# Conditioning projections of a two-layer decoder step: raw float32 slabs in four TensorE column groups in place of split slabs over the whole array

## The chip, the core and the metric

The kernel runs as one program on one core of a Trainium2 chip. The metric is the device time of one execution in microseconds (us). The engines are named as the profile names them: PE is TensorE (PEld its weight loads), DVE is VectorE, ACT is ScalarE, POOL is GpSimd, and SP is the queue that issues most DMAs. A number such as L649 is a line of the kernel before.

## What is computed

One inference step of a decoder trunk with D = 1024, for a prompt of 512 tokens and 8 single-token samples, hence 520 token columns and 9 sequences (each with its own conditioning vector c). Layer 0 mixes tokens with a gated linear recurrence of 8 heads (HGRN2), layer 1 with latent attention over a shared latent. Around each mixer stand two half-step SwiGLU networks of inner width 2816. Every sub-layer is an RMS norm whose shift, scale and gate come from c:

```
sc = jax.nn.silu(c)
for l in range(DEPTH):
    if l == N_A_LAYERS:
        ckv, krope = shared_kv(x, sc, pos, kv_w_ada, kv_b_ada, ...)     # its own shift and scale, 2 x D columns
    mods = (sc @ w_ada[l] + b_ada[l]).reshape(Bn, 3, 3, D)[:, :, :, None, :]
    def mod(y, j):
        return rmsnorm(y, g_norm[l, j]) * (1 + mods[:, j, 1]) + mods[:, j, 0]
    x = x + 0.5 * mods[:, 0, 2] * swiglu(mod(x, 0), w_ffn_gu[l, 0], w_ffn_down[l, 0])
    h = mod(x, 1)
    ...                                    # y = HGRN2 (layer 0) or latent attention (layer 1)
    x = x + mods[:, 1, 2] * y
    x = x + 0.5 * mods[:, 2, 2] * swiglu(mod(x, 2), w_ffn_gu[l, 1], w_ffn_down[l, 1])
```

The conditioning projections `sc @ w_ada[l]` (9 x 1024 columns in each layer) and `sc @ kv_w_ada` (2 x 1024 columns) are what is changed. They read 80 MiB of the weights for a result of 9 rows.

## The kernel before

**Slabs.** All weights are float32 and come through a ring of four buffers, `raw` (`RAW` = 4), in slabs of up to 2048 words in each of 128 partitions, 1 MiB (1.05 MB). SP issues the two DMAs of a slab (L408) once the slab four places earlier has been multiplied (`slot_used`). ACT then makes `w_hi`, the slab rounded to the float32r type, and DVE makes `w_lo`, what is left of it (L1239, L1635). Both run `AHEAD` = 2 slabs ahead of the multiplication: handling slab k they first split slab k + 2. ACT waits for the landing there, and everything behind that wait on ACT waits with it.

**Large products.** The activations are split the same way (`hn_hi`, `hn_lo`, `hid_hi`, `hid_lo`). A 128 x 128 weight tile is multiplied with 520 columns in two halves of 260, each in three passes, hi x hi, hi x lo and lo x hi (L627 to L629).

**Conditioning slabs (`ada`).** There are 80: 36 of each `w_ada[l]` and 8 of `kv_w_ada`, each 256 columns wide with all 1024 rows. silu(c) stands in `sc18`, 128 partitions x 8 chunks x 18 columns, high part of the 9 sequences beside the low part. One slab takes 16 matmuls of 256 moving columns (L649 with `w_hi`, L650 with `w_lo`), which accumulate 18 rows in PSUM bank 6. ACT copies the rows to `rows` (L1247), and `ada_comb` on PE (L661) adds the two parts and turns the rows to columns by two matmuls against a constant. DVE adds the bias into `mods` (L1643). So each slab has its own rows copy, turn and bias step.

**Where they stand.** 14 slabs (`ADA_FIRST`) go in front of the first norm. One stands behind each of the 22 hidden chunks of the two networks of layer 0 (its turn lies in the next hidden chunk, between gate and up). Two go with each of the 8 heads' projections, which run interleaved with the recurrence of the head before (`hgrn_events`). The last 6 go with the head norms, which run in the last head's recurrence (`last_events`, `hgrn_norm`). The two networks of layer 1 have none. The order on each engine is written out by hand; the engines run the same list of events and meet at semaphores.

## Time and profile before

| what | value |
|---|---|
| median of 3 runs | 2860.28 us |
| range | 2857.2 to 2860.41 us |
| span of the profiled execution | 2860.2 us |
| PE busy / DVE / ACT | 92% / 45% / 31% |
| PE's share of the chain that ended last | 84% |
| mean granted clock, share of full speed | 0.958 |
| moved by DMA | 294.25 MB, mean 103 GB/s |

The profile is of one execution, and its span equals the median to 0.1 us. Its busy times of PE add overlapping records, since matmuls are pipelined: what one costs is seen from the distance between starts, not from its own duration. A float32 matmul (not float32r) leaves two weight-load records and two matmul records.

### The profile page before, as it was taken

How to read it: one execution, taken by the hardware profiler on the slowest of the kernel's cores; microseconds unless marked ns; L12 is line 12 of the kernel's file. 1: busy time of each engine (PE TensorE's matmuls, PEld its weight loads, DVE VectorE, ACT ScalarE, POOL GpSimd, SP SyncE). 2: the span in 40 equal slices, each digit the busy share in tenths (PEclk: the TensorE clock that was granted, in tenths of full speed). 3: DMA queues.
4: the chain of work that ended last, by engine and by line, in shares of the span. 5: the costliest groups of instructions: out<-in, count | busy, mean ns of one | idle time of the engine just before them, and what ended most of it. 6: DMA issues, size and time to landing. Idle time of an engine off the chain costs nothing.

```text
span 2860.2 us, 48702 instructions
## 1 busy us (share of the span) xinstructions
PE 2621.6 (92%) x20002; PEld 2407.8 (84%) x20002; DVE 1296.3 (45%) x1975; ACT 881.4 (31%) x1034; POOL 38.2 (1%) x64
## 2 busy tenths in 40 slices
PE   5799999899998689999987999996888999899997
PEld 4799999899998589999987999996763437899997
DVE  5544344556566854434446333345452223533333
ACT  4533133433334243313325212124333222321212
POOL 1000000000000000000000000000000000000000
PEclk9899999999999699999998999998999998999998
DMA  8344353333444125434432323221023332223321
GB/s 270 111 148 142 108 153 122 104 108 104 120 119 140 60 81 152 143 104 140 136 107 59 99 78 100 78 89 28 27 85 88 88 91 59 74 81 95 91 75 57
DMA packets 412517, 294.25 MB, mean 103 GB/s; under 512 B 35557, under 2 KB 408380, under 8 KB 412384
## 3 DMA queue, kind: packets, MB, share of 16 engines
q1 hardware_dynamic: 407456, 277.14, 32.6%
q0 software_dynamic: 4928, 15.30, 1.7%
q8 instruction: 88, 1.44, 0.2%
q14 instruction: 45, 0.37, 0.0%
HBM read 284.87 MB, written 7.51 MB: 102 GB/s over the span
## 4 chain that ended last, share of the span: by engine, by line
PE 84%; DVE 7%; ACT 3%; DMA 2%; issue 2%; SPq 1%; POOL 0%; DVEq 0%; ACTq 0%; POOLq 0%
PE ps L627 22%; PE ps L628 22%; PE ps L629 22%; PE ps L649 2%; PE ps L650 2%; PE ps L1173 2%; PE ps L870 2%; PE ps L1132 2%; PE ps L661 1%; PE ps L1133 1%; DMA raw<-in_hg_w_in 1%; DMA raw<-in_w_ada 1%; DVE rstd L1694 1%; DVE rstd L1899 1%; PE ps L1106 1%
## 5 line engine op out<-in xcount | busy, mean ns | idle before, releaser
L627 PE MATMUL ps<-hn_hi,w_hi 128*128 128x260 f32 x3680 | 1066.1, 290 | 49.4 <-DVE hn_lo L1710 47.1
L629 PE MATMUL ps<-hn_hi,w_lo 128*128 128x260 f32 x3680 | 1051.5, 286 | 0.0
L628 PE MATMUL ps<-hn_lo,w_hi 128*128 128x260 f32 x3680 | 1050.6, 285 | 0.0
L627 PEld LDWEIGHTS ps<-hn_hi,w_hi 128*128 128x128 f32 x3680 | 706.3, 192 | 55.4 <-issue 51.6
L1635 DVE TENSOR_TENSOR w_lo<-raw,w_hi 128x2048 fp32r<-128x2048 f32 (+5 forms) x280 | 564.3, 2016 | 316.7 <-ACT w_hi L1239 316.6
L629 PEld LDWEIGHTS ps<-hn_hi,w_lo 128*128 128x128 f32 x3680 | 706.0, 192 | 0.0
L628 PEld LDWEIGHTS ps<-hn_lo,w_hi 128*128 128x128 f32 x3680 | 705.8, 192 | 0.0
L1239 ACT ACTIVATE w_hi<-raw 128x2048 fp32r<-128x2048 f32 (+3 forms) x273 | 472.7, 1732 | 491.8 <-DMA raw<-in_w_ffn_gu 220.8
L628 PE MATMUL ps<-hid_lo,w_hi 128*128 128x260 f32 x1408 | 398.7, 283 | 0.0
L627 PE MATMUL ps<-hid_hi,w_hi 128*128 128x260 f32 x1408 | 397.9, 283 | 0.0
L629 PE MATMUL ps<-hid_hi,w_lo 128*128 128x260 f32 x1408 | 397.8, 283 | 0.0
L1723 DVE TENSOR_TENSOR hf<-ps,sg 128x520 f32<-128x520 f32 x88 | 61.6, 700 | 487.4 <-PE ps L629 487.4
L629 PEld LDWEIGHTS ps<-hid_hi,w_lo 128*128 128x128 f32 x1408 | 265.1, 188 | 0.0
L627 PEld LDWEIGHTS ps<-hid_hi,w_hi 128*128 128x128 f32 x1408 | 264.9, 188 | 0.1
L628 PEld LDWEIGHTS ps<-hid_lo,w_hi 128*128 128x128 f32 x1408 | 264.4, 188 | 0.0
L1311 ACT ACTIVATE sg<-ps 128x520 f32<-128x520 f32 x88 | 52.6, 597 | 394.2 <-PE ps L629 394.2
L649 PE MATMUL ps<-w_hi,sc 128*18 128x256 f32 x640 | 158.3, 286 | 0.5 <-DVE x L1942 0.5
L650 PE MATMUL ps<-w_lo,sc 128*18 128x256 f32 x640 | 156.6, 284 | 0.0
L1737 DVE TENSOR_TENSOR t<-ps,gate 128x8 f32<-128x8 f32 x80 | 13.4, 167 | 255.6 <-PE ps L629 255.6
L1282 ACT ACTIVATE sq<-x 128x520 f32<-128x520 f32 x56 | 35.5, 638 | 253.8 <-DVE x L1742 212.9
L1247 ACT ACTIVATE rows<-ps 18x256 f32<-18x256 f32 x80 | 29.4, 368 | 240.0 <-PE ps L650 240.0
L870 PE MATMUL ps<-qs,kk 128*128 128x128 f32 x512 | 74.4, 292 | 26.7 <-DVE qs L1857 16.9
(289 smaller groups left out, 2357.4 us busy)
## 6 DMA issues: line engine op xcount, KB each, us to landing
raw<-in_w_ffn_gu SPq DMA_DIRECT2D x176, 512.0 KB
raw<-in_w_ada SPq DMA_DIRECT2D x144, 512.0 KB
raw<-in_w_ffn_down SPq DMA_DIRECT2D x96, 384.0 KB
raw<-in_hg_w_in SPq DMA_DIRECT2D x32, 512.0 KB
pg<-in_cache_ckv SPq DMA_DIRECT2D x128, 128.0 KB, 2.0
raw<-in_w_ffn_down SPq DMA_DIRECT2D x32, 256.0 KB
raw<-in_kv_w_ada SPq DMA_DIRECT2D x16, 512.0 KB
ss<-in_state_hgrn POOLq DMA_DIRECT2D x8, 512.0 KB, 7.1
```

The costliest lines, as they stand in the source:

```text
L627: pe.matmul(out[:, t, :], wh, xh[:, c], start=start, stop=False)
L628: pe.matmul(out[:, t, :], wh, xl[:, c], start=False, stop=False)
L629: mm = pe.matmul(out[:, t, :], wl, xh[:, c], start=False, stop=stop)
L649: pe.matmul(ps[0:18, 6, 0:ADA_W], sc18[:, k, :], hi[:, k, :], start=(k == 0), stop=False)
L650: mm = pe.matmul(ps[0:18, 6, 0:ADA_W], sc18[:, k, :], lo[:, k, :], start=False, stop=(k == 7))
L870: mm = pe.matmul(out[:, s], kk[:, q, s], qs[:, q, s], start=True, stop=True)
L1132: pe.matmul(o, qsamp[:, q, r, :], cts[g % 2][:, r, :], start=(r == 0), stop=False)
L1173: pe.matmul(ps[0:H, 3, 0:KV], pts[:, p, :], pg[q][:, p, :], start=(p == 0), stop=False)
L1239: act.activation(w_hi[:, r, 0:n], raw[r][:, 0:n], ACT.Copy).then_inc(hi_done, 1)
L1311: act.activation(two(sg[:, T.n.get("up", 0) % 2, :]), pair[0], ACT.Silu).then_inc(gate_read, 1)
L1635: ins = dve.tensor_tensor(w_lo[r][:, c], raw[r][:, c], w_hi[:, r, c], ALU.subtract)
L1723: dve.tensor_tensor(two(hf[:]), pair[1], two(sg[:, T.n.get("up", 0) % 2, :]), ALU.mult).then_inc(up_read, 1)
```

## The change

The 80 conditioning slabs are no longer split. A slab is now 256 rows (`ADA_K` = 2 chunks of 128) by all 1024 columns of one of the 20 blocks of D columns, four slabs to a block. PE multiplies the landed `raw` slab itself, in float32, as soon as it has landed: for each of the two chunks four matmuls, one for each quarter of 256 columns. Each uses 32 columns of the array (`tile_position=(0, g * 32)`) and writes the 32 PSUM partitions of its group, all in bank 6. The stationary operand `scz` holds silu(c) in 9 of 32 columns and zeros in the rest. After the fourth slab ACT copies 128 x 256 `rows` once, PE turns them by two 128 x 128 transposes, and DVE adds the bias in two instructions. The placement is new too: 8 slabs (two blocks, shift and scale) in front of the first norm in place of 14; 20 in each network of layer 0 (`ADA_ROUNDS`, rounds of four hidden chunks with a slab behind each); 20 in the HGRN stage (4 with head 0's projection, then 2 with each head's, and 2 with head norms in place of 6); 12 in the first network of layer 1. The gate is no longer made in `norm` but by `make_gate` ahead of the first down product and of the output projection. The diff, cut:

```diff
+ADA_K = 2
+ADA_S = KD // ADA_K
 ADA_W = 256
-ADA_L = 9 * D // ADA_W
+CG = 4
+GW = P // CG
...
+ADA_FIRST = 2
+ADA_ROUNDS = {(0, 0): (3, 2), (0, 1): (3, 2), (1, 0): (3, 0), (1, 1): (0, 0)}
...
+    def ffn(l, j):
         out = []
-        for mn in (MFA, MFB):
-            out += [SLOT] * (mn * (2 if with_ada else 1)) + [mn // 2 * 256] * 8
+        for mn, rounds in zip((MFA, MFB), ADA_ROUNDS[l, j]):
+            out += [SLOT, 0] * (ADA_S * rounds) + [SLOT] * (mn - ADA_S * rounds) + [mn // 2 * 256] * 8
         return out
-    return ([SLOT] * ADA_FIRST + ffn(True) + [SLOT] * (4 * H + ADA_TAIL + 4) + ffn(True) + [SLOT, KD * P] + ffn(False)
-            + [SLOT, KD * P] + [QK * 384, RK * 256, RK * 256] * 4 + [RK * D] + [SLOT] * 4 + ffn(False))
+    hgrn = [SLOT, 0, 0, SLOT, 0, 0] + [SLOT, 0, SLOT, 0] * 7 + [0] * 2
+    return ([0] * (ADA_S * ADA_FIRST) + ffn(0, 0) + hgrn + [SLOT] * 4 + ffn(0, 1) + [SLOT, KD * P] + ffn(1, 0)
+            + [SLOT, KD * P] + [QK * 384, RK * 256, RK * 256] * 4 + [RK * D] + [SLOT] * 4 + ffn(1, 1))
...
+def hgrn_events(project, slab=None):
 
 
     t = (lambda a, n: [("tiles", a, n)]) if project else (lambda a, n: [])
-    ada = (lambda j: [("ada", j, 0)]) if project else (lambda j: [])
-    comb = (lambda j: [("comb", j, 0)]) if project else (lambda j: [])
+    ada = (lambda j: [("ada", slab + j, 0)]) if slab is not None else (lambda j: [])
...
-    return [("fresh", 0, 16), ("ada", 0, 0), ("tiles", 16, 8), ("comb", 0, 0), ("tiles", 24, 8), ("ada", 1, 0),
-            ("comb", 1, 0)]
+    return [("fresh", 0, 16), ("ada", 0, 0), ("ada", 1, 0), ("tiles", 16, 16), ("ada", 2, 0), ("ada", 3, 0),
+            ("comb", 0, 0)]
...
-        sc18 = place("sc18", [P, KD, 2 * SEQS], F32R)
+        scz = place("scz", [P, KD, GW])
...
-        rows = place("rows", [2 * SEQS, ADA_W])
+        rows = place("rows", [P, ADA_W])
...
+            def ada(view, col, s):
+
+                columns(view, col, D, ADA_K * s, ADA_K)
...
+            for j in range(ADA_FIRST):
+                for s in range(ADA_S):
+                    ada(ada_v[0], j * D, s)
+            ffn(0, 0, ada_v[0], ADA_FIRST * D)
+            for g in range(2):
+                hgrn_project(0, 2 * g)
+                ada(ada_v[0], 7 * D, 2 * g)
+                ada(ada_v[0], 7 * D, 2 * g + 1)
...
+            def ada(slab):
+
+                k0 = T.n.get("slot", 0)
+                turns = LAND * (k0 // RAW + 1)
+                if T.i is not None:
+                    turns = T.i * (LAND * T.per["slot"] // RAW) + turns
+                pe.wait_ge(landed[k0 % RAW], turns)
+                if slab == 0 and (T.n.get("ada", 0) or T.i is not None):
                     pe.wait_ge(rows_copied, T.at("ada"))
-                split()
-                for k in range(KD):
-                    pe.matmul(ps[0:18, 6, 0:ADA_W], sc18[:, k, :], hi[:, k, :], start=(k == 0), stop=False)
-                    mm = pe.matmul(ps[0:18, 6, 0:ADA_W], sc18[:, k, :], lo[:, k, :], start=False, stop=(k == 7))
+                w = raw[k0 % RAW][:].rearrange("p (k n) -> p k n", k=ADA_K)
+                for kk in range(ADA_K):
+                    k = ADA_K * slab + kk
+                    for g in range(CG):
+                        mm = pe.matmul(ps[g * GW:(g + 1) * GW, 6, 0:ADA_W], scz[:, k, :],
+                                       w[:, kk, g * ADA_W:(g + 1) * ADA_W], start=(k == 0), stop=(k == KD - 1),
+                                       tile_position=(0, g * GW))
                 mm.then_inc(slot_used, 1)
                 T.add("slot")
-                T.add("ada")
+                if slab == ADA_S - 1:
+                    T.add("ada")
...
-                    mm = pe.matmul(ps[:, 7, j * SEQS:(j + 1) * SEQS], rows[:, j * P:(j + 1) * P], comb,
-                                   start=True, stop=True)
+                    mm = pe.transpose(ps[:, 7, j * P:(j + 1) * P], rows[:, j * P:(j + 1) * P], ident)
...
+            def ffn(l, j):
+
+
+                due = False
                 for half, mn in ((0, MFA), (1, MFB)):
-                    by_hand = 2 if with_ada else mn % 4 or 4
+                    rounds = ADA_ROUNDS[l, j][half]
+                    if rounds:
+                        for m in range(ADA_S):
+                            hidden(half == 0 and m == 0, due and m == 0, m == 0)
+                            ada(m)
+                        due = True
+                        with T.loop(pe, rounds - 1, {"slot": 2 * ADA_S, "lo": ADA_S, "up": ADA_S, "ada": 1, "comb": 1}):
+                            for m in range(ADA_S):
+                                hidden(False, m == 0)
+                                ada(m)
...
+                if n:
+                    r = k % RAW
+                    turns = LAND * (k // RAW + 1)
+                    if T.i is not None:
+                        turns = T.i * (LAND * T.per["split"] // RAW) + turns
+                    act.wait_ge(landed[r], turns)
+                    act.activation(w_hi[:, r, 0:n], raw[r][:, 0:n], ACT.Copy).then_inc(hi_done, 1)
...
+            def ada(slab):
                 split_hi()
-                act.wait_ge(slot_used, T.at("slot", 1))
-                if T.n.get("ada", 0):
-                    act.wait_ge(comb_done, T.at("ada"))
-                act.activation(rows[:], ps[0:2 * SEQS, 6, 0:ADA_W], ACT.Copy).then_inc(rows_copied, 1)
+                if slab == ADA_S - 1:
+                    act.wait_ge(slot_used, T.at("slot", 1))
+                    if T.n.get("ada", 0) or T.i is not None:
+                        act.wait_ge(comb_done, T.at("ada"))
+                    act.activation(rows[:], ps[:, 6, 0:ADA_W], ACT.Copy).then_inc(rows_copied, 1)
+                    T.add("ada")
...
+                for b in range(2):
+                    cols = mods[:, bass.ds(col, 8), :].rearrange("p (g b) s -> p g b s", b=2)
+                    added = bias[:, bass.ds(col, 8)].rearrange("p (g b) -> p g b", b=2)
+                    ins = dve.tensor_tensor(cols[:, :, b, :],
+                                            ps[:, 7, b * P:(b + 1) * P].rearrange("p (g s) -> p g s", g=CG)[:, :, 0:SEQS],
+                                            added[:, :, b].unsqueeze(2).broadcast_to([P, CG, SEQS]), ALU.add)
+                ins.then_inc(mods_added, 1)
...
+            def make_gate(base, factor):
+
+                dve.wait_ge(mods_added, T.at("comb"))
+                if T.n.get("res", 0):
+                    dve.wait_ge(x_upd, T.at("res", 2, 2))
+                link(dve.tensor_scalar(gate[:], mods[:, base:base + KD, :].rearrange("p c s -> p (c s)"), factor, None,
+                                       ALU.mult))
...
-                if h < ADA_TAIL:
-                    split_lo()
-                    T.add("slot")
+                if h < 2:
+                    ada_slot()
...
-                if h < ADA_TAIL:
-                    add_mods(C_L1 + 2 * (H + h))
+                if h == 1:
+                    add_mods(C_L1)
```

PE's order from the start to the first norm. `raw_52` to `raw_55` are the four buffers of the ring, `sc_66` is `sc18`, `rows` is the copied rows. Before (the first of 14 slabs and its turn):

```order
L945 MATMUL ps<-cst,xr 128x128 x32
L948 MATMUL ps<-cst,xs 128x8 x8
L649 MATMUL ps<-w_hi,sc_66 18x256
L650 MATMUL ps<-w_lo_56,sc_66 18x256
L649 MATMUL ps<-w_hi,sc_66 18x256
L650 MATMUL ps<-w_lo_56,sc_66 18x256
```

After:

```order
L954 MATMUL ps<-cst,xs 128x8 x8
L661 MATMUL ps<-raw_52,scz 32x256 x8
L661 MATMUL ps<-raw_53,scz 32x256 x8
L661 MATMUL ps<-raw_54,scz 32x256 x8
L661 MATMUL ps<-raw_55,scz 32x256 x8
L675 MATMUL ps<-cst,rows 128x128 x2
L661 MATMUL ps<-raw_52,scz 32x256 x8
L661 MATMUL ps<-raw_53,scz 32x256 x8
L661 MATMUL ps<-raw_54,scz 32x256 x8
L661 MATMUL ps<-raw_55,scz 32x256 x8
L675 MATMUL ps<-cst,rows 128x128 x2
L694 MATMUL ps<-rstd,ones 128x260 x2
```

Sixteen matmuls a slab with a turn behind each have become eight a slab with a turn behind each fourth, and the sums of the first norm (L694) follow the eighth slab.

ACT's order in the projection of head 0, where a slab is split (`w_hi`), and the sigmoids of the projection are taken. Before:

```order
L1363 ACTIVATE sgq<-ps 128x520
L1366 ACTIVATE s_110<-ps 128x520
L1367 ACTIVATE s_111<-ps 128x520
L1239 ACTIVATE w_hi<-raw_53 128x2048
L1247 ACTIVATE rows<-ps 18x256
L1239 ACTIVATE w_hi<-raw_54 128x2048
L1371 ACTIVATE vv<-ps 128x520
```

After:

```order
L1357 ACTIVATE sgq<-ps 128x520
L1360 ACTIVATE s_109<-ps 128x520
L1361 ACTIVATE s_110<-ps 128x520
L1249 ACTIVATE w_hi<-raw_53 128x2048
L1365 ACTIVATE vv<-ps 128x520
L1368 ACTIVATE sgg<-ps 128x520
L1249 ACTIVATE w_hi<-raw_52 128x2048
L1258 ACTIVATE rows<-ps 128x256
```

Before, the split behind the sigmoids was that of a conditioning slab, and head 0's second projection slab had been split ahead of `sgq`; now that second slab is split behind the sigmoids.

DVE's order around the head norms in the last head's recurrence. Before:

```order
L1667 TENSOR_TENSOR hn_lo<-fg,hn_hi 128x520
L1643 TENSOR_TENSOR mods<-ps,bias 128x18
L1853 TENSOR_TENSOR tot<-tot 128x64
L1855 TENSOR_TENSOR kk<-kk,tot 128x64x4
L1857 TENSOR_TENSOR qs<-qs,tot 128x64x4
L1859 COPY_PREDICATED attn<-lmask,ps 128x512
L1635 TENSOR_TENSOR w_lo_59<-raw_55,w_hi 128x2048
L1899 RECIPROCAL rstd<-kk 128x520
```

After:

```order
L1660 TENSOR_TENSOR hn_lo<-fg,hn_hi 128x520
L1839 TENSOR_TENSOR tot<-tot 128x64
L1841 TENSOR_TENSOR kk<-kk,tot 128x64x4
L1843 TENSOR_TENSOR qs<-qs,tot 128x64x4
L1845 COPY_PREDICATED attn<-lmask,ps 128x512
L1884 RECIPROCAL rstd<-kk 128x520
```

The split and the bias step between two head norms are gone.

## Rows read from the trace of the kernel before

**Rows 1.** The page: span, and the chain that ended last by engine.
```profile
span 2860.2 us, 48702 instructions
...
PE 84%; DVE 7%; ACT 3%; DMA 2%; issue 2%; SPq 1%; POOL 0%; DVEq 0%; ACTq 0%; POOLq 0%
```

**Rows 2.** Weight loads by line: name, xcount | busy us, mean ns | idle before.
```profile
L649 PEld LDWEIGHTS ps<-w_hi,sc 128*18 128x18 f32 x640 | 62.8, 98 | 13.5 <-DVE x L1942 0.6
```

**Rows 3.** PE's timeline, first network: start us, duration us, name.
```profile
121.17 0.28 PE L629 MATMUL ps<-hn_hi,w_lo 128*128 128x260 f32 x1
121.38 0.61 PE L661 MATMUL ps<-cst,rows 18*128 18x9 f32 x4
121.92 0.39 PE L627 MATMUL ps<-hn_hi,w_hi 128*128 128x260 f32 x1
...
127.67 0.28 PE L629 MATMUL ps<-hn_hi,w_lo 128*128 128x260 f32 x1
127.78 0.28 PE L649 MATMUL ps<-w_hi,sc 128*18 128x256 f32 x1
...
129.64 0.28 PE L627 MATMUL ps<-hn_hi,w_hi 128*128 128x260 f32 x1
...
135.46 0.39 PE L661 MATMUL ps<-cst,rows 18*128 18x9 f32 x2
```

**Rows 4.** ACT's timeline in layer 1's first network, gate sigmoids of two hidden chunks.
```profile
1575.95 0.61 ACT L1311 ACTIVATE sg<-ps 128x520 f32<-128x520 f32 x1 [8.88 <-PE ps L629]
...
1587.43 0.60 ACT L1311 ACTIVATE sg<-ps 128x520 f32<-128x520 f32 x1 [9.07 <-PE ps L629]
```

**Rows 5.** L1173: ns min/median/max; then PE's timeline there, and transposes.
```profile
L1173 PE MATMUL ps<-pg,pts x256: 379/379/634, 2161.3 to 2376.9; 128*8 128x256 f32 x128
...
2161.28 1.89 PE L1173 MATMUL ps<-pg,pts 128*8 128x256 f32 x8 [0.41 <-ACT pts L1586]
...
2169.84 1.88 PE L1132 MATMUL ps<-ct,qsamp 128*8 128x512 f32 x4
2171.65 1.02 PE L1133 MATMUL ps<-ct,qsamp 64*8 64x512 f32 x2
...
2172.88 0.27 PE L1122 MATMUL ps<-cst,pgk 128*64 128x128 f32 x1
2172.99 0.38 PE L1121 MATMUL ps<-cst,pg 128*128 128x128 f32 x2
```

**Rows 6.** PE's timeline, first conditioning slab and first matmul of the first network.
```profile
28.77 0.29 PE L649 MATMUL ps<-w_hi,sc 128*18 128x256 f32 x1 [0.49 <-DVE x L1942]
...
99.41 0.56 PE L627 MATMUL ps<-hn_hi,w_hi 128*128 128x260 f32 x1 [7.39 <-DVE hn_lo L1710]
```

**Rows 7.** ACT's timeline in front of the first norm: fifth and last split of a slab.
```profile
36.11 1.91 ACT L1239 ACTIVATE w_hi<-raw 128x2048 fp32r<-128x2048 f32 x1 [1.83 <-DMA raw<-in_w_ada]
...
78.63 1.91 ACT L1239 ACTIVATE w_hi<-raw 128x2048 fp32r<-128x2048 f32 x1 [2.20 <-DMA raw<-in_w_ada]
```

**Rows 8.** Stretches, the last three columns: granted clock, DMA share, GB/s.
```profile
15.00:20.00 5.00, 0.00 (x0) 0.00 (x0) 0.74 (x5) 4.09 (x8) 0.00 (x0) 1.00 1.05 396
...
30.00:82.00 52.00, 38.69 (x271) 28.90 (x269) 31.16 (x27) 29.87 (x29) 0.00 (x0) 0.90 0.85 267
```

**Rows 9.** A head's step: DVE's split, then the PE matmul behind it.
```profile
648.84 2.29 DVE L1635 TENSOR_TENSOR w_lo<-raw,w_hi 128x2048 fp32r<-128x2048 f32 x1 [0.70 <-ACT w_hi L1239]
...
652.16 0.37 PE L870 MATMUL ps<-qs,kk 128*128 128x128 f32 x1 [1.59 <-DVE qs L1857]
```

**Rows 10.** Head 0's projection: ACT behind the sigmoids, PE behind the projection.
```profile
565.38 1.92 ACT L1239 ACTIVATE w_hi<-raw 128x2048 fp32r<-128x2048 f32 x1
...
564.19 0.28 PE L649 MATMUL ps<-w_hi,sc 128*18 128x256 f32 x1
...
581.75 0.66 PE L862 MATMUL ps<-cst,vv 128*128 128x128 f32 x4
```

**Rows 11.** The chain that ended last, last head's step: start us, us, what.
```profile
925.54 2.17 DVE w_lo L1635
```

353 lines of the change are left out of this document (139 added, 214 removed).

## Prediction

> **What bounds the kernel now.** I began with the chain that ended last: PE is 84% of it and DVE 7%, in a span of 2860.2 us [rows 1]. So what PE spends on a conditioning slab is time, except where PE waits for something else. The timeline of PE in a network of layer 0 gives the price. From one turn (L661) to the next a hidden chunk with its slab takes 135.46 - 121.38 = 14.08 us [rows 3]. In layer 1, where no slabs are, one gate sigmoid follows the other after 1587.43 - 1575.95 = 11.48 us [rows 4]. A slab thus costs 2.60 us there. The parts: around the sixteen matmuls the start moves by 129.64 - 127.67 = 1.97 us, of which 0.12 is the ordinary step, so 1.85; around the turn by 121.92 - 121.17 = 0.75, so 0.63; the last 0.12 is loop and refill. Three places are bound otherwise. In front of the first norm the weights arrive too slowly: DMA is busy 0.85 of 30 to 82 us, and ACT splits wait for landings [rows 7, 8]. In a head's step PE waits 1.59 us for a level operand which DVE makes behind a 2.29 us split of a conditioning slab [rows 9]. In the last head's step the chain runs on DVE itself, with a 2.17 us split in each round [rows 11].
>
> **The price of the new slab (X).** Nothing in this trace runs on 32 columns at a time, so I bound it. A plain float32 matmul of 256 moving columns leaves two records. Eight such records take 1.89 us, the last of them 0.38, so they start 0.216 apart; with 512 columns it is 0.43 [rows 5]. One matmul is 0.43 us, eight are 16 records = 3.45 us if nothing overlaps. If all four groups run together it is a quarter, 0.86. To either I add 0.2 for entering and leaving another shape of the array: from four records of 0.43 on 128 rows to the next on 64 rows it is 2171.65 - 2169.84 = 1.81, hence 0.1 a change [rows 5]. X lies between 1.06 and 3.65. I take a value between the ends. PE starts its records in program order, in every row that I read, and a group's second record (same 32 columns, other weights) must wait for its first. Then the next group's first record runs beside this group's second, and no more: 2 records at a time, 9 steps of 0.215 for a slab, 1.93, so **X = 2.13 us**.
>
> The Trainium skill, "TensorE: Matmul & The Clock Gate", Part 3 on packing small matmuls, has column tiles start about 4 ns apart and reports 2.38 times for three of them; it also says that matmuls never leave program order. Its first statement taken alone gives the lower end (a rival below), the second gives my value, and no row here shows column tiles at all. "TensorEngine Tiling (Array Packing)", Key Properties, says that a change of tiling mode drains the array; the 0.1 us agrees.
>
> **The turn.** Before, 80 turns of 0.63. After, 20, each with two transposes. A transpose is one record, 0.11 to the next (2172.99 - 2172.88) [rows 5]; four records became two, 0.63 - 0.22 = 0.41.
>
> **Front.** The first slab starts at 28.77, behind the transposes of x, not behind weights [rows 6]. Four slabs lie in the ring by then. The fifth landed at 36.11, 5.5 us after the first slab was used up at 30.6, and the sixteenth at 78.63: 3.87 us each [rows 7]. The first norm's last rows wait for that landing, since ACT splits slab 16 ahead of copying them. Now the ninth slab (the first network's first) is the one that ACT splits before the second rows copy. It lands between 30 + 5.5 + 4 x 2.7 = 46 (1.05 MB at the 396 GB/s of 15 to 20 us [rows 8], larger pieces) and 36.1 + 4 x 3.87 = 51.6. That is 27 to 32 us earlier than 78.63; I take **-30**. X hardly matters (3.65 would make it -25). Behind it the norm is as before, down to the first matmul at 99.41 [rows 6]; the next slabs have those 20 us to land. If x lands later, because the slabs' larger pieces take more of the DMA engines, up to 3 us are lost.
>
> **The two networks of layer 0 and the first of layer 1.** 44 slabs at 2.60 = 114.4 go. 52 slabs at X = 110.8 and 13 turns at 0.41 = 5.3 come, 12 of the slabs where none were. Together **+2**. Splits, rows copies and bias steps lie under PE's work: a chunk leaves ACT idle 9 of 11.48 us [rows 4]. If X were 1.06 this term is -54, at 3.65 it is +80: it decides the sign.
>
> **Seven head steps.** Each loses 2 x 1.85 + 2 x 0.63 + the wait of 1.59 (DVE has no split ahead of the level any more [rows 9]) = 6.55, and gains 2X + 0.2 (a turn in every other step) = 4.46. 7 x -2.1 = **-15**. If the level wait stays for another reason it is -4.
>
> **Head 0's projection.** Now 581.75 - 564.19 = 17.6 us [rows 10]. After: PE has two slabs to do behind the first half, but the second half's split comes only behind the sigmoids: ACT 565.38 + 1.92, DVE 2.29 more, so 569.6, 5.4 us after 564.19, longer than 2X. Then 96 matmuls of 0.12 = 11.5, two slabs 4.3, rows copy and turn 1.6 (nothing covers them): 22.8. **+5**.
>
> **Last head's step.** Four of the splits on DVE go, 4 x 2.17 = 8.7 [rows 11], with them bias steps and PE's slabs, turns and rows copies between the early norms; 9 to 20, I take **-12**. Of `make_gate`: one small DVE operation that moves from the norm to a place where DVE waits for PE, nothing.
>
> Sum: -30 + 2 - 15 + 5 - 12 = -50, **2810 us**. The profiled span and the median are the same to 0.1 us.
>
> **Rivals.**
> - *All four groups at once.* X = 1.06. For it: no row forbids it, if the records of different groups need not wait for each other. Against it: program order with two records a matmul. -31 - 54 - 30 + 3 - 12 = -124, 2736 us.
> - *No overlap.* If the groups share the path of the moving data, X = 3.65. For it: in each row read, one matmul starts only when the one before has streamed. Front -25, networks +80, steps 7 x (7.5 - 6.55) = +7, head 0 +10, last head -10: +62, 2922 us. This is the case on the other side. Each 0.1 us of X is worth about 7 us over the 72 slabs outside the front, so it decides from X = 2.13 + 50 / 70 = 2.8 us on.
> - *Two at a time, but each step shows its weight load.* A load of few columns takes 98 ns [rows 2], hidden today by the matmul before. Nine of them in the open: X = 3.0. -27 + 48 - 2 + 7 - 11 = +15, 2875 us.
> - *The change does not shorten the front*, as some other arrival holds the first network: the forecast loses most of its 30, 2840 us.
>
> **How the numbers follow.** Two at a time (with or without a few us of the front) 0.48; four at a time 0.20; weight loads in the open 0.10; no overlap 0.20; the rest 0.02. The range must leave out no more than 0.2: I leave out the case without overlap, and reach from a little below 2736 to a little above 2875, 2730 to 2885. The forecast's own range is 2790 to 2832, from the front (27 to 32), the level wait (11) and the last head (9 to 20). A measurement of this kernel tells about 0.2% (6 us). Faster by more: 0.20 + 0.45 + 0.02 = 0.67; within it 0.05, from the upper edge of the forecast and the lower edge of open loads; slower 0.28.
>
> **What would show it.** Right: in the first network a hidden chunk with its slab takes 11.48 + 2.1 to 2.3 = 13.6 to 13.8 us, 13.9 to 14.1 with a turn; a slab's records overlap in pairs and its sixteen starts span about 1.7 us (0.65 with four at a time, 3.2 with none); the first matmul of the first network starts near 69 us, not 99; no rows copy between most head norms. Wrong: starts 0.215 apart over a whole slab; a clock that falls behind the slabs; a wait of PE for `raw` in the networks; a head step that is no shorter because DVE's next operation comes as late as the split did.

## The result, and the profile after

The changed kernel takes 2766.07 us (median of 4 runs, 2762.28 to 2766.92) against 2860.35 us of the kernel before on the same chip: a ratio of 0.9671, 95% interval 0.9657 to 0.9685, or 94 us less. The forecast was 2810, its range 2730 to 2885. The sign and the range held; half of the gain was missing from the sum, and two of its terms were wrong in opposite directions.

The page of the kernel after, its span and the chain that ended last by engine and by line (L633 to L635 are now the three matmuls of a weight tile, L661 the conditioning matmul):

```profile
span 2764.9 us, 47021 instructions
...
PE 84%; DVE 7%; ACT 3%; DMA 2%; issue 2%; SPq 1%; POOL 0%; DVEq 0%; ACTq 0%; POOLq 0%
PE ps L633 23%; PE ps L635 22%; PE ps L634 22%; PE ps L661 2%; PE ps L1182 2%; PE ps L875 2%; PE ps L1141 2%; DMA raw<-in_hg_w_in 1%; PE ps L1142 1%; ACT w_hi L1249 1%; DVE rstd L1690 1%; DVE rstd L1884 1%; PE ps L1115 1%; PE ps L1096 1%; PE ps L911 1%
```

By engine the chain is word for word that of before [rows 1]. So the page alone does not tell where 95 us of span went. I read it off at places that both kernels have, by starts on PE (a "head step" is one head's recurrence with the next head's projection):

| stretch | before | after | difference |
|---|---|---|---|
| start to the first network matmul | 99.41 | 67.67 | -31.7 |
| first network of layer 0 and the norm behind it | 450.45 | 419.08 | -31.4 |
| head 0's projection, norm to the turned values | 31.9 | 36.9 | +5.0 |
| seven head steps with a projection | 316.1 | 313.8 | -2.3 |
| last head's step | 93.3 | 79.9 | -13.4 |
| output projection and norm | 60.6 | 60.9 | +0.3 |
| second network of layer 0 | 450.4 | 418.8 | -31.6 |
| latent projection, first network of layer 1 | 436.0 | 450.8 | +14.8 |
| the rest | 922.0 | 917.1 | -4.9 |

**The slab.** PE's timeline of the kernel after around one slab in the first network, and the next one a chunk later (start us, duration us, line, operands):

```profile
208.41 0.28 PE L635 MATMUL ps<-hn_hi,w_lo 128*128 128x260 f32 x1
208.62 1.07 PE L661 MATMUL ps<-raw,scz 128*32 128x256 f32 x16
209.62 0.39 PE L633 MATMUL ps<-hn_hi,w_hi 128*128 128x260 f32 x1
...
221.32 1.07 PE L661 MATMUL ps<-raw,scz 128*32 128x256 f32 x16
```

Sixteen records take 1.07 us. The matmul behind the slab starts 1.21 us after the one ahead of it, of which 0.12 is the ordinary step: X is 1.09. A hidden chunk with a slab takes 221.32 - 208.62 = 12.70 us, 1.22 more than one without [rows 4]; it was 2.60 more. With a turn it takes 12.93.

Of the slab's records, those that start from 208.60 to 208.65 are these:

```profile
208.62 0.42 PE L661 MATMUL ps<-raw,scz 128*32 128x256 f32 x4
```

Four records start within 0.05 us, and the next four follow 0.24 us later. I read them as the first and the second record of each column group, side by side all the time; a record does not name its group, so this rests on E7 and E8.

**The head steps.** A head's recurrence has levels, each of which needs operands from DVE. In the kernel before PE waited at two of them in a step. At level 4, behind the split of a conditioning slab, it was 1.51 to 1.59 us in every step, the wait of [rows 9]. At level 5, behind the split of the next head's network slab, it was 1.95, 1.08, 0.81 and 0.68 us in four of the six steps looked at below and nothing in two. Here is the second wait in the step of [rows 9], DVE and PE of the kernel before:

```profile
654.21 2.29 DVE L1635 TENSOR_TENSOR w_lo<-raw,w_hi 128x2048 fp32r<-128x2048 f32 x1 [1.54 <-ACT w_hi L1239]
...
658.15 1.05 PE L870 MATMUL ps<-qs,kk 128*128 128x128 f32 x7 [1.08 <-DVE attn L1859]
```

In the kernel after the wait at level 4 is gone from every step, and the one at level 5 is 3.7 to 4.1 us in all six. PE, then DVE, then ACT and SP of the kernel after, in one head's step:

```profile
550.99 0.28 PE L635 MATMUL ps<-hn_hi,w_lo 128*128 128x260 f32 x1
555.21 0.46 PE L875 MATMUL ps<-qs,kk 128*128 128x128 f32 x2 [3.94 <-DVE attn L1845]
```

```profile
546.20 0.72 DVE L1845 COPY_PREDICATED attn<-lmask,ps 128x512 f32<-128x512 uint32 x1
551.25 2.29 DVE L1634 TENSOR_TENSOR w_lo<-raw,w_hi 128x2048 fp32r<-128x2048 f32 x1 [4.33 <-ACT w_hi L1249]
553.46 0.17 DVE L1839 TENSOR_TENSOR tot<-tot 128x16 f32<-128x16 f32 x1
```

```profile
543.62 0.60 ACT L1361 ACTIVATE s<-ps 128x520 f32<-128x520 f32 x1
549.31 1.91 ACT L1249 ACTIVATE w_hi<-raw 128x2048 fp32r<-128x2048 f32 x1 [5.09 <-DMA raw<-in_hg_w_in]
```

```profile
543.11 1.03 SPq L411 DMA_DIRECT2D raw<-in_hg_w_in  x2
```

Read it from the bottom. SP may fill the slot of the next head's first network slab only when the slab four places earlier, this head's own, is used up: PE's last matmul with it starts at 542.80, and SP issues the load at 543.11. ACT stands idle for 5.09 us until it lands, 6.2 us after the issue. DVE waits for ACT, splits for 2.29 us, and only then makes the level's operands (L1839 and on). PE waits 3.94 us for these. From the issue to PE's matmul at level 5 it is 12.1 us. In the kernel before it was 12.1 and 12.9 us in two steps (issues at 646.07 and 598.54, matmuls at 658.15 and 611.47). The change leaves this chain as long as it was and takes away the PE work that lay beside it.

### The profile page after: what moved, and what is told of

Read it like the earlier page. It is cut to its first block, busy times and chain, and to the rows that moved or that the text cites. A ratio compares the mean times of both kernels' runs of the same rounds, so it can differ in the third digit from the quotient of the medians.

```text
span 2764.9 us, 47021 instructions
## 1 busy us (share of the span) xinstructions
PE 2513.7 (91%) x19722; PEld 2279.6 (82%) x19722; DVE 1114.6 (40%) x1854; ACT 709.9 (26%) x893; POOL 38.0 (1%) x64
## 4 chain that ended last, share of the span: by engine, by line
PE 84%; DVE 7%; ACT 3%; DMA 2%; issue 2%; SPq 1%; POOL 0%; DVEq 0%; ACTq 0%; POOLq 0%
PE ps L633 23%; PE ps L635 22%; PE ps L634 22%; PE ps L661 2%; PE ps L1182 2%; PE ps L875 2%; PE ps L1141 2%; DMA raw<-in_hg_w_in 1%; PE ps L1142 1%; ACT w_hi L1249 1%; DVE rstd L1690 1%; DVE rstd L1884 1%; PE ps L1115 1%; PE ps L1096 1%; PE ps L911 1%
## 5 line engine op out<-in xcount | busy, mean ns | idle before, releaser
L633 PE MATMUL ps<-hn_hi,w_hi 128*128 128x260 f32 x3680 | 1069.1, 291 | 53.9 <-DVE hn_lo L1706 47.1
L635 PE MATMUL ps<-hn_hi,w_lo 128*128 128x260 f32 x3680 | 1052.5, 286 | 0.0
L633 PEld LDWEIGHTS ps<-hn_hi,w_hi 128*128 128x128 f32 x3680 | 707.3, 192 | 79.7 <-issue 72.3
L635 PEld LDWEIGHTS ps<-hn_hi,w_lo 128*128 128x128 f32 x3680 | 706.9, 192 | 0.0
L1634 DVE TENSOR_TENSOR w_lo<-raw,w_hi 128x2048 fp32r<-128x2048 f32 (+5 forms) x200 | 381.4, 1908 | 436.1 <-ACT w_hi L1249 435.9
L1249 ACT ACTIVATE w_hi<-raw 128x2048 fp32r<-128x2048 f32 (+4 forms) x193 | 319.8, 1657 | 766.3 <-DMA raw<-in_w_ffn_gu 509.4
L633 PE MATMUL ps<-hid_hi,w_hi 128*128 128x260 f32 x1408 | 398.5, 283 | 0.0
L635 PE MATMUL ps<-hid_hi,w_lo 128*128 128x260 f32 x1408 | 397.3, 282 | 0.0
L633 PEld LDWEIGHTS ps<-hid_hi,w_hi 128*128 128x128 f32 x1408 | 264.7, 188 | 1.2 <-issue 1.2
L635 PEld LDWEIGHTS ps<-hid_hi,w_lo 128*128 128x128 f32 x1408 | 265.2, 188 | 0.0
L1311 ACT ACTIVATE sg<-ps 128x520 f32<-128x520 f32 x88 | 52.3, 594 | 313.8 <-PE ps L635 313.8
L875 PEld LDWEIGHTS ps<-qs,kk 128*128 128x128 f32 x512 | 71.4, 215 | 57.8 <-DVE qs L1843 42.3
L661 PE MATMUL ps<-raw,scz 128*32 128x256 f32 x1280 | 87.9, 396 | 5.9 <-DMA raw<-in_w_ada 4.8
L1736 DVE SCALAR_TENSOR_TENSOR x<-ps,gate,x 128x260 f32<-128x260 f32 (+1 forms) x160 | 70.1, 480 | 2.8
```

The source lines that it names most:

```text
L633: pe.matmul(out[:, t, :], wh, xh[:, c], start=start, stop=False)
L635: mm = pe.matmul(out[:, t, :], wl, xh[:, c], start=False, stop=stop)
L661: mm = pe.matmul(ps[g * GW:(g + 1) * GW, 6, 0:ADA_W], scz[:, k, :], w[:, kk, g * ADA_W:(g + 1) * ADA_W], start=(k == 0), stop=(k == KD - 1 ...
L875: mm = pe.matmul(out[:, s], kk[:, q, s], qs[:, q, s], start=True, stop=True)
L1249: act.activation(w_hi[:, r, 0:n], raw[r][:, 0:n], ACT.Copy).then_inc(hi_done, 1)
L1311: act.activation(two(sg[:, T.n.get("up", 0) % 2, :]), pair[0], ACT.Silu).then_inc(gate_read, 1)
```

## Experiments

Each experiment edits the kernel after. E1 to E3 and E5 each move one thing, E4 and E6 a group of things; E7, E8, E10 and E11 each measure one price, and E9 joins E5 and E7. The medians of the kernel before, taken beside them, lie between 2855.86 and 2861.74 us, so a difference of a few us between medians of two experiments says little. "Step" below is one of the six head steps from head 1's `sgq` on ACT to head 7's. All six together, in a view of that stretch (length, busy us of PE, PEld, DVE, ACT, POOL, then granted clock, DMA share, GB/s), before and after:

```profile
589.97:866.26 276.29, 262.48 (x2150) 255.91 (x2149) 168.21 (x325) 90.63 (x138) 14.12 (x18) 0.97 0.40 116
```

```profile
534.69:808.89 274.20, 251.25 (x2108) 241.00 (x2107) 140.61 (x307) 66.44 (x117) 14.10 (x18) 0.95 0.37 117
```

PE is busy 11 us less and DVE 28 us less, and 2 us came of it. PE's idle time grew from 13.8 to 22.95 us, and its clock cost more: 0.97 of full speed over 276.29 us is about 8 us lost, 0.95 over 274.20 at most 14 (some of it while PE waited anyway, which leaves about 13). Six other runs with the same code in these steps (E2 to E4, E8, E10, E11) took 272.3 to 275.2 us.

### E7: all four matmuls in one column group

```diff
-                        mm = pe.matmul(ps[g * GW:(g + 1) * GW, 6, 0:ADA_W], scz[:, k, :],
+                        mm = pe.matmul(ps[0:GW, 6, 0:ADA_W], scz[:, k, :],
                                        w[:, kk, g * ADA_W:(g + 1) * ADA_W],
-                                       start=(k == 0), stop=(k == KD - 1), tile_position=(0, g * GW))
+                                       start=(k == 0 and g == 0), stop=(k == KD - 1 and g == CG - 1),
+                                       tile_position=(0, 0))
```

> The four matmuls of a k step all go to column group 0 and add up there, with 32 columns of weights as before; the sum of the four column ranges stands where one of them should, so the modulations are not those of the reference. The work on the arrays is the same but for the overlap. Theory 'four groups run at once': a slab in the open costs 1.09 us now because 16 records of 0.22 us or more overlap four at a time; in one group it costs 16 x 0.22 = 3.5 to 3.8 us, so the 52 slabs of the networks add 125 to 140 us and those of HGRN up to 50: 2890 to 2950 us. Rival 'two records of one matmul overlap anyway, groups give a factor of two only': about 2 us a slab, 2766 + 47 + up to 18 = 2813 to 2835. Rival 'no overlap, the records are short': 2766.

Measured: 2917.86 us, 152 more than the kernel after. PE's timeline around a slab:

```profile
210.85 0.28 PE L635 MATMUL ps<-hn_hi,w_lo 128*128 128x260 f32 x1
211.06 3.64 PE L661 MATMUL ps<-raw,scz 128*32 128x256 f32 x16
214.63 0.39 PE L633 MATMUL ps<-hn_hi,w_hi 128*128 128x260 f32 x1
```

Same operands, same count, same shapes; without the groups X is 214.63 - 210.85 - 0.12 = 3.66, with them 1.09. The ratio is 3.4 and not 4; the 0.2 us for entering and leaving, if both have them, explain that (3.46 / 0.89 = 3.9). 52 slabs in the networks at 2.57 each are 134 of the 152 us, and the front is 7.3 us longer (first network matmul at 75.00). In one group the records start 0.22 us apart ((3.64 - 0.38) / 15), never together, so it is the groups that make a slab shorter by 2.57 us. The theory of four at once holds. The run also shows what the prediction's rival "no overlap" (3.65) would have been.

The head steps say something else. Six of them at 3.66 us a slab:

```profile
594.16:871.59 277.43, 270.20 (x2108) 244.40 (x2107) 141.07 (x307) 66.50 (x118) 14.10 (x18) 1.00 0.38 115
```

277.4 us against 274.2, though twelve slabs cost 31 us more of PE. The wait at level 5 is shorter:

```profile
660.54 0.71 PE L875 MATMUL ps<-qs,kk 128*128 128x128 f32 x4 [1.14 <-DVE attn L1845]
```

1.14 us in place of 3.94. That takes in one of the step's two slabs. The other is paid by the clock, which now stands at 1.00 throughout. Over the six steps PE's idle time falls from 22.95 to 7.23 us, 15.7 less. The clock takes nothing where it took about 13. The rest, 3.2 us, is what the stretch grew. So between X = 1.09 and X = 3.66 a slab costs little in these steps, because a longer one fills a wait whose end the slab does not set, and spares the slow clock behind that wait.

### E8: the k steps of a group one behind the other

```diff
-                for kk in range(ADA_K):
-                    k = ADA_K * slab + kk
-                    for g in range(CG):
+                for g in range(CG):
+                    for kk in range(ADA_K):
+                        k = ADA_K * slab + kk
```

> In a slab the loops are exchanged: for each column group its two k steps follow each other (0,0,1,1,2,2,3,3 rather than 0,1,2,3,0,1,2,3); same arithmetic, same operands. If TensorE takes matmuls strictly in program order and a matmul waits while its own group is busy, a group's four records of 0.22 us follow one another and only the last of one overlaps the first of the next: 13 x 0.22 + 0.12 = about 3.0 us a slab, 2766 + 52 x 1.9 + up to 30 = 2865 to 2895 us. If it starts a later group's matmul ahead of one that waits, the slab stays near 1.09 us: 2762 to 2770. Program order with two records of a matmul spread over groups (the reading of the trace after the change): between, two pairs at a time, 1.7 to 2.2 us: 2800 to 2830.

Measured: 2773.04 us (2771.66 and 2774.41), X = 1.11. PE in the window from 209.25 to 209.30, then the matmul behind the slab:

```profile
209.25 0.44 PE L661 MATMUL ps<-raw,scz 128*32 128x256 f32 x4
...
210.27 0.39 PE L633 MATMUL ps<-hn_hi,w_hi 128*128 128x260 f32 x1
```

The program now has group 0 twice, group 1 twice and so on, with two records each. Still four records start at once, and the slab ends 1.02 us after its start (1.00 in the kernel after). Taken strictly in program order it would have needed about 3 us, the estimate above. A matmul that waits for its own column group does not hold back a later one for another group. The records don't name their group; that the four are of four groups is inferred from the length. Since in E7 no two records of one group start together, and the whole slab takes 1.02 us, I see no other reading. The four starts are also a little further apart here than in the kernel after (four records together 0.44 us long against 0.42). The Trainium skill, "TensorE: Matmul & The Clock Gate", Part 2, has matmuls always stay in program order. Across column groups this run speaks against it, and my forecast leaned on the same idea. The 7 us in the whole time are not the slabs (80 x 0.02 = 1.6): up to the query projection of layer 1 the run is 1.2 us ahead (1846.58 against 1847.77), and the attention behind it is 6 us longer, of which more at E3 and E4.

### E1: the split of the next head's slab behind tile 26

```diff
-                        if j % 16 == 0:
+                        if j in (0, 26) or n == 16:
                             split_hi()
...
-                        if j == 16 or kind == "fresh":
+                        if j == 26 or n == 16:
                             split_lo()
```

> Only change: in the seven head steps that project, the split of the next head's first slab (w_hi on ScalarE, w_lo on VectorE) stands behind tile 26, between the turned keys and the state, and no longer ahead of tile 16. Theory 'landing chain': after the change each of these steps waits 3.9 to 4.4 us at level 5, because VectorE's level work stands in order behind a split whose slab has landed only then (PE L635 at 550.99, L875 at 555.21). With the split later that wait goes and TensorE's own work bounds the step: six loop steps and the one after them lose about 4 us each, the stage from 523.65 to 837.42 (313.8 us) falls to 284 to 292, the whole time to 2738 to 2746 us. Rival 'VectorE is late anyway': the level work of VectorE and ScalarE is the bound whatever is split where, the wait moves to the keys or the state: the stage stays within 4 us of 313.8, the whole at 2762 to 2768. Rival 'the split is only moved into another wait': a wait of about 2 us opens at the keys or the state, the whole at 2748 to 2756.

Measured: 2752.36 us (ratio to before 0.9638, 0.9619 to 0.9658). Six steps take 257.99 us, 16 less than after; the theory had 22 to 30 for seven. The wait at level 5 is gone in each, and a new one stands at L903, the head's output, where PE needs the state:

```profile
600.45 0.38 PE L903 MATMUL ps<-attn,vn 128*128 128x128 f32 x2
602.99 0.49 PE L903 MATMUL ps<-attn,vn 128*128 128x128 f32 x2 [2.16 <-DVE st L1854]
```

```profile
599.29 2.29 DVE L1634 TENSOR_TENSOR w_lo<-raw,w_hi 128x2048 fp32r<-128x2048 f32 x1 [2.69 <-ACT w_hi L1249]
601.50 0.28 DVE L1852 COPY st<-ps 128x128 f32<-128x128 f32 x1
```

The rival "only moved into another wait", with its 2748 to 2756, had it right. The landing is no longer in the way, but DVE still splits ahead of work that PE waits for.

### E5: w_hi ahead of tile 24, w_lo behind the state

```diff
-                        if j % 16 == 0:
+                        if j in (0, 24) or n == 16:
                             split_hi()
...
-                        if j == 16 or kind == "fresh":
+                        if j == 28 or n == 16:
                             split_lo()
```

> As the run with the split behind tile 26, but ScalarE's half (w_hi) stands ahead of tile 24 and VectorE's half (w_lo) behind the state, ahead of tile 28. In the run before, the waits of 4 us at level 5 went, and one of 2.16 us came at L903 in each step, where TensorE waits for the state that VectorE makes behind w_lo (w_lo at 599.29, state 601.50). Theory 'any split that stands in order ahead of work that TensorE waits for costs a wait': now the state comes first, neither wait is left, a step of 42 to 43.6 us falls by another 2.1 us, and FFN(0,1) starts some 13 us earlier than at 959.63; whole time 2737 to 2745 us. Rival: the slab's landing or w_lo is then late for the next head's first tile (w_lo done about 4 us before it at best) and the wait of about 2 us moves there: 2750 to 2754.

Measured: 2732.16 us, ratio 0.9560 (0.9544 to 0.9576): 34 us less than the kernel after, by the order of two instructions a step. That is 5 us better than the best of the 2737 to 2745 expected. The six steps:

```profile
530.26:768.21 237.95, 237.95 (x2108) 229.01 (x2107) 141.77 (x307) 66.48 (x118) 14.10 (x18) 1.00 0.43 134
```

PE is busy in all of the 237.95 us. A step is 39.66 us where it was 45.70 after and 46.05 before. That is 6.04 us less than after, and more than the 3.8 us of waits that a step had (22.95 / 6), so I looked at the clock. Kernel after, the same view in short windows across one wait:

```profile
545.00:551.00 6.00, 6.00 (x54) 6.00 (x52) 1.89 (x5) 1.69 (x1) 0.00 (x0) 1.00 1.04 333
551.00:555.20 4.20, 0.27 (x3) 0.08 (x2) 3.91 (x6) 1.25 (x5) 0.00 (x0) 1.00 0.01 2
555.20:557.00 1.80, 1.79 (x14) 1.80 (x15) 1.47 (x7) 0.00 (x0) 0.00 (x0) 0.86 0.00 0
557.00:559.00 2.00, 2.00 (x11) 2.00 (x11) 0.97 (x2) 0.26 (x1) 0.00 (x0) 0.50 0.00 0
559.00:561.00 2.00, 2.00 (x15) 2.00 (x15) 0.70 (x3) 0.35 (x1) 0.00 (x0) 0.77 0.00 0
561.00:563.00 2.00, 2.00 (x19) 2.00 (x18) 0.89 (x2) 0.60 (x1) 0.00 (x0) 1.00 0.00 0
```

The third number from the end is the granted clock. PE waits from 551 to 555.2, and behind the wait the mean clock of three stretches is 0.86, 0.50 (that is 1.2 GHz, the lower of its two levels) and 0.77 of full speed, while PE is busy throughout. The first and the third mix full and half speed: in stretches of 0.5 us it is still 1.00 up to 556.2, 0.50 from 556.7 to 559.7, and 1.00 again from 560.2. What is lost: 1.80 x 0.14 + 2.00 x 0.50 + 2.00 x 0.23 = 1.7 us. At two of the six waits the clock falls a little before the wait ends and stays low longer, and about 3 us are lost. Over all six it is at most 0.05 x 274.20 = 13.7 us, and about 12.6 without what fell into the waits, 2.1 a step. With the 3.8 of the wait that makes 5.9 of the 6.04. In E1, too, the wait of 2.16 us in each step came with a mean clock of 0.97.

### E9: one column group, with E5's order of splits

The edits of E7 and E5 together.

> The one-group kernel (all four matmuls of a k step into column group 0, 3.66 us a slab; wrong modulations) with the head steps' split moved as in the run with w_hi ahead of tile 24 and w_lo ahead of tile 28. In the seven head steps a slab's price did not show while the landing chain bound them: 45.3 to 46.6 us a step at 1.21 us a slab, 46.1 to 46.4 at 3.66. Theory: with the split late TensorE bounds the step, and the price shows in full: 39.65 + 2 x 2.45 = 44.5 us a step, the whole at 2918 - 7 x 1.7 = 2906, range 2900 to 2912. Rival 'something else than TensorE paces the 39.65 us': the step stays near 40 to 42, the whole at 2885 or less.

Measured: 2912.24 us; the steps:

```profile
593.54:862.24 268.70, 268.70 (x2108) 244.04 (x2107) 142.20 (x307) 65.93 (x117) 14.10 (x18) 1.00 0.39 119
```

44.78 us a step against E5's 39.66: 5.12, or 2 x 2.56, the full price of two slabs, both at a clock of 1.00. Together the four runs are a square. With the split early, X costs 0.5 us a step (45.70 and 46.24), for the wait and the slow clock take in the rest; with the split late it costs all (39.66 and 44.78). The whole time is at the upper edge of the 2900 to 2912 expected.

### E2: head 0's slabs in another order

```diff
-    return [("fresh", 0, 16), ("ada", 0, 0), ("ada", 1, 0), ("tiles", 16, 16), ("ada", 2, 0), ("ada", 3, 0),
+    return [("fresh", 0, 16), ("ada", 0, 0), ("tiles", 16, 16), ("ada", 1, 0), ("ada", 2, 0), ("ada", 3, 0),
```

> Only change: head 0's projection takes its slabs in the order network, conditioning, network, conditioning x3, so that the second network slab's split stands ahead of the sigmoids on ScalarE and VectorE. Theory: TensorE's wait of 3.45 us at 506.00 in the kernel after the change (for w_lo of that slab, split behind the sigmoids) goes; head 0's projection 500.61 to 523.65 (23.0 us) falls to about 19.5, the whole time by 3 to 4 us to about 2762.5. Rival: the three conditioning slabs in a row at the end wait for their landing instead (each 1 MB, and a slab of the network has to be loaded in the same time), and nothing is gained: 2765 to 2768.

Measured: 2766.14 us, nothing gained. The wait of 3.45 us for the second half went, and one of 5.59 us came at the end:

```profile
522.29 0.69 PE L676 MATMUL ps<-cst,rows 128*128 128x128 f32 x2 [5.59 <-ACT rows L1259]
```

```profile
520.06 1.91 ACT L1250 ACTIVATE w_hi<-raw 128x2048 fp32r<-128x2048 f32 x1 [5.45 <-DMA raw<-in_hg_w_in]
521.88 0.37 ACT L1259 ACTIVATE rows<-ps 128x256 f32<-128x256 f32 x1
```

The slab that lands at 520.06 is head 1's. It is loaded when the slab four places ahead of it is used, which in the new order is the second half itself. The ring's depth decides here, as in the rival, though through the network's slab and not the conditioning ones. (The order of SP's loads and the list of slots follow the same edit.)

### E3 and E4: the front

E3 lets ACT copy the second block's rows ahead of splitting the first network slab. E4 leaves copy and split as they are in the kernel after, and puts the squares of x and their sum ahead of the slabs, root and reciprocal between the two blocks, since they need x alone. ACT's part of both edits (DVE's order follows it, and in E4 PE's):

```diff
-            for _ in range(ADA_FIRST):
+            for j in range(ADA_FIRST):
                 for s in range(ADA_S):
+                    if j == ADA_FIRST - 1 and s == 2:
+                        act.wait_ge(slot_used, T.at("slot", 2))
...
+                        break
                     ada(s)
             for c in range(KD):
                 x_square(c, (x_placed, KD + 1))
+            split_hi()
+            split_hi()
```

```diff
+            for c in range(KD):
+                x_square(c, (x_placed, KD + 1))
-            for _ in range(ADA_FIRST):
+            for j in range(ADA_FIRST):
                 for s in range(ADA_S):
                     ada(s)
-            for c in range(KD):
-                x_square(c, (x_placed, KD + 1))
-            norm(C_L0)
+                if j == 0:
+                    x_root_of()
+            norm(C_L0, False)
```

> Only change: at the front, the split of the first network slab stands behind the copy of the second conditioning block's rows and the squares of x on ScalarE, and behind the sum of squares on VectorE. Theory: the copy of the rows no longer waits for that slab's landing (L1249 at 46.67 after an idle of 14.70 us; the copy at 48.48, PE's turn 48.90, though PE's last slab ends at about 44.8). The turn comes at about 45.4 and the first network matmul at 63.9 to 64.5 rather than 67.67: the whole falls by 3 to 4 us to about 2762.5. Rival: the squares and their sum (L1282, L1672), then root and reciprocal, are what is long here, and VectorE's split of 2.29 us now stands in front of the reciprocal: gain 1 to 2 us.

> Only change: the squares of x, their sum, its root and reciprocal stand ahead of the projection's slabs of the front (root and reciprocal between its two column blocks); they need x alone. Theory 'the front of the new kernel is a chain, no longer a transfer': between the last slab (44.8) and the first network matmul (67.67) stand 22.9 us, of which squares 48.75 to 56.3, root 60.32, reciprocal 61.05 to 64.48 are independent of the projection. With them ahead, the first network matmul comes at about 54 to 55: whole time 2751 to 2754 us. Rival 'the transfers bound the front': the first slab of the network (landed at 46.67) and the ring behind it are late too, and the gain is given back as waits in the first networks' slabs: less than 6 us gained, 2760 or more.

Measured: E3 2763.56 us (2759.5 to 2768.89), E4 2757.23 us (2753.53 to 2760.95). The first network matmul starts at 63.35 in E3, 4.3 earlier, and at 55.10 in E4, 12.6 earlier; close to what the theories had (63.9 to 64.5, and 54 to 55). E4's whole time is above its 2751 to 2754. ACT in E4:

```profile
38.11 0.69 ACT L1290 ACTIVATE root<-ps,eps 128x520 f32<-128x520 f32 x1 [1.36 <-PE ps L697]
47.23 1.91 ACT L1250 ACTIVATE w_hi<-raw 128x2048 fp32r<-128x2048 f32 x1 [8.43 <-DMA raw<-in_w_ffn_gu]
49.05 0.37 ACT L1259 ACTIVATE rows<-ps 128x256 f32<-128x256 f32 x1
```

In both runs the gain is still there at the query projection of layer 1 (1842.64 and 1831.28, where the kernel after has 1847.77; most of the 3.9 us that E4 has won on the way lie in its HGRN stage, 3.6 us shorter). Then the stage of attention takes 513.4 and 513.1 us, where it took 507.8 in the profile after and 509.6 before. Neither edit touches that stage. Over the eight samples the view gives, after and E4:

```profile
2050.00:2290.00 240.00, 218.28 (x1046) 90.37 (x1044) 53.47 (x134) 69.60 (x96) 0.00 (x0) 0.96 0.29 81
```

```profile
2034.00:2280.00 246.00, 222.38 (x1055) 93.40 (x1053) 54.27 (x135) 70.06 (x97) 0.00 (x0) 0.94 0.29 79
```

The granted clock is 0.96 in one and 0.94 in the other. From the start of the last copy of scores in one sample (`srow` on ACT) to the first in the next it is 17.1 to 19.1 us after and 17.0 to 20.4 in E4; E2 has the same row of gaps as the kernel after. Over all the profiles, before included, the stage was 507.8 to 514.2 us long, with no relation to the edit. What sets it stays open. It is why effects of 5 us are read from the place of the first network matmul here and not from a median. That place itself is 66.9 to 68.7 us in the kernel after and the five runs whose front is the same (E1, E2, E5, E8, E10).

### E11: twelve slabs in front of the norm

```diff
-ADA_FIRST = 2
-ADA_ROUNDS = {(0, 0): (3, 2), ...
+ADA_FIRST = 3
+ADA_ROUNDS = {(0, 0): (3, 1), ...
```

> 12 conditioning slabs in front of the first norm rather than 8, four fewer in the first FFN's second half. Theory 'transfers pace the front': at 0.35 to 0.41 MB a microsecond four more slabs of 1 MB take 10.5 to 12 us, and the first network matmul comes at 78 to 80 instead of 67.67; four slabs and a turn fewer in the network give back 4 x 1.22 + 0.23 = 5.1: whole 2771 to 2773. Rival 'TensorE's slabs are what takes the time': 4 x 1.09 = 4.4 us more at the front, nothing in all: 2765 to 2767.

Measured: 2773.36 us. The first network matmul starts at 78.85, 11.2 us later, and ACT's split of the first network slab shows why:

```profile
57.85 1.91 ACT L1250 ACTIVATE w_hi<-raw 128x2048 fp32r<-128x2048 f32 x1 [12.00 <-DMA raw<-in_w_ffn_gu]
```

In the kernel after it starts at 46.67. Four slabs more, 11.18 us more: 2.8 us each, 375 GB/s. PE's 4 x 1.09 us do not show. The front is paced by transfers up to this landing and by a chain of small operations behind it. The first network gives back 3.6 us of the 5.1 expected.

### E10: a split's worth of VectorE work in four head norms

```diff
+                if 2 <= h < 6:
+                    link(dve.tensor_reduce(t9[:, 0, 0:1], x[:, 0:4, :].rearrange("p c t -> p (c t)"), AX_X, ALU.max))
```

> Added: in the head norms 2 to 5 VectorE makes one more operation over 128 x 2080 elements (a maximum over x, about 2.2 us, into a scratch cell), in the place where the kernel before had its split of a conditioning slab. Theory of the last-head term: VectorE's row of operations (reciprocal 3.40 us in each norm) sets this end, so the four cost about 4 x 2.2 = 9 us, and last head's step to the first output-projection matmul (79.85 us) becomes 87 to 89: whole 2773 to 2776. Rival: there is slack in norms 2 to 5 (they lie among the last head's levels), 0 to 3 us: 2766 to 2769.

Measured: 2773.23 us. One of the four:

```profile
886.22 2.30 DVE L1882 TENSOR_REDUCE t<-x 128x1 f32<-128x2080 f32 x1
```

From the last tile of the last projection to the first of the output projection it is 89.7 us against 80.3: +9.4, for 4 x 2.30 = 9.2 us of work. DVE sets this end, and what is added to its work there is paid in full. That what it is spared is saved in full is the same argument turned round.

### E6: all that helped, together

E5's order of splits; at the front E3's and E4's orders, with DVE's w_lo of the first network slab inside the norm, behind the sample columns:

```diff
                         split_act(ts[:], hn_hi[:, :, NP:NT], hn_lo[:, :, NP:NT])
+                        for _ in range(splits):
+                            split_lo()
...
-            norm(C_L0, V_NORM)
+            norm(C_L0, V_NORM, False, 2)
```

> The split of the run above, and at the front: squares, sum, root and reciprocal ahead of the last rows, the copy of the rows ahead of the first network slab's split, and VectorE's w_lo of that slab inside the norm. Expected from the single runs: first network matmul at 51 to 52 (67.67 in the kernel after the change, 55.10 with the statistics first), head steps as in the run above (-30 in all against the kernel after the change). Sum -16 -31: 2766 - 47 = 2719, range 2715 to 2728, since the attention of the sample group alone moves by 5 us between runs of one kernel. Rival: earlier networks meet transfers that are not earlier (the gain at the front is given back in the first networks): 2732 or more.

Measured: 2720.49 us (5 runs, 2715.24 to 2721.8), ratio to before 0.9513, 0.9498 to 0.9528; the expected sum was 2719. It is the fastest kernel here, 46 us below the kernel after. The first network matmul:

```profile
53.20 0.56 PE L633 MATMUL ps<-hn_hi,w_hi 128*128 128x260 f32 x1 [6.79 <-DVE hn_lo L1720]
```

That is 14.5 us earlier than after, not the 16 expected: w_lo sits in the norm's own row on DVE, so it delays the first hn_lo. The first network loses none of it (419.1 us with its norm, as after).

## Why the prediction was right, and where it was not

**The price of the slab.** This is the step that failed: "PE starts its records in program order", from which followed that "the next group's first record runs beside this group's second, and no more: 2 records at a time". That a group's second record waits for its first is true: they are 0.22 to 0.24 us apart. That others wait behind it is not, across column groups: by E8 a later group's matmul starts ahead of one that waits. So X is 1.09 and not 2.13; the lower bound, 0.86 + 0.2 = 1.06, was right to 0.03, though its two parts, 0.86 and 0.2, were not measured apart. E7 gives the upper bound as well, 3.66 where the text had 3.65. Both ends came from rows of other shapes [rows 5]; only the choice between them was wrong, since every row behind it showed one matmul after another on the same columns, and such rows can't tell whether order or occupation makes one wait. The rival "all four groups at once" had 0.20.

**The networks.** With a slab and a turn at what they cost here: 52 x 1.22 + 13 x 0.23 = 66.4 against 114.4, -48; the three stretches of the table give -31.4 - 31.6 + 14.8 = -48.2. Forecast +2; the rival had -54. The turn was 0.23 rather than 0.41, worth 2 us.

**The front.** -30 forecast, -31.7 measured. Its mechanism was right too: the first network slab lands at 46.67 (46 to 51.6 foreseen), ACT splits it ahead of the copy of the rows, and E11 shows a slab there to cost 2.8 us of transfer and none of PE. With X = 3.66 (E7) it is 7.3 us longer, where the text had 5.

**The seven head steps.** -15 forecast, -2.3 measured; and with X = 1.09 the same sum would have said 7 x (2 x 1.09 + 0.2 - 6.55) = -29. The wait of 1.59 did go, at level 4, as forecast. The step that failed is the reason given for it, "DVE has no split ahead of the level any more": it holds for level 4 and not for level 5, where DVE still splits the next head's network slab first. The wait there was left out of the sum. It was 0.75 us a step on average before (13.8 us of idle time in six steps, less six waits of 1.51 to 1.59), because PE's longer slabs filled most of the time until that slab was split. With short slabs PE comes to level 5 earlier and waits 3.8. The clock is the second term that the sum left out: it took about 1.4 us a step before and 2.1 to 2.3 after. By the forecast's own prices with X = 1.09 a step is 4.2 us shorter. The longer wait gives back 3.1 and the clock 0.7 to 0.9, which leaves 0.2 to 0.4; 0.35 was measured. E7 and E9 show that the term was right as a price (5.12 us for 2 x 2.57, E9 against E5) and wrong as a saving. The reading that would have caught it was at hand: the last sentence of "What would show it" names "a head step that is no shorter because DVE's next operation comes as late as the split did". I asked what DVE does ahead of the level, but not when the slab behind that split can land, with a ring of four and a release that this change does not move.

**Head 0's projection.** +5 forecast, +5.5 by the same two places. The second half waits 3.45 us for w_lo behind the sigmoids, as worked out. E2 shows that the other order does not avoid it with this ring.

**Last head's step.** -12 forecast, -13.4 measured, and E10 supports the reason: DVE's work there counts one for one. That covers the four splits, 8.7 us; no run takes the other 4.7 apart.

**The sum.** The errors were +2 instead of -48 and -15 instead of -2. They partly cancel, 50 against 13, and that is luck. The range held because it was drawn out to the rival "all four groups at once"; the forecast's own range, 2790 to 2832, did not hold. With the right X and all else as reasoned the sum is -30 - 48 - 29 + 3 - 12 = -116, 2744 us, 22 too low; with the head steps at -2 and head 0 at +5 it is -87, 2773. Of the 7 us between that and the 2766 measured, 5 lie behind the first network of layer 1, where neither kernel has a conditioning slab: 1.8 in the attention, 3.1 behind it. In those last 410 us both kernels have the same 3216 matmul records and PE waits alike, but it is busy 393.9 us before and 390.9 after, at a mean clock of 0.97 and 0.98. That is the clock, and not the change's doing as far as the rows show.

## What to carry to other kernels

When a change makes a step shorter, look for the operation in it whose start is set by something the change does not move (here a landing in a ring of four), follow who stands behind it in order on each engine, and expect the saving to stop there; then move that operation behind everything others wait for. List every wait of the stage, not only the longest: here the shorter one was the one that grew. Sixteen records with small stationary operands cost 1.09 us in four column groups and 3.66 in one, whatever the order in which the groups are written. A wait of TensorE of 3.8 us was worth 6 us here, since the clock drops behind it.
